# Stick-breaking attention with queries on partitions: a running product along the keys in place of logarithms and a triangle product

## The chip, the cores and the metric

One core of a Trainium2 chip. The metric is the device time of one launch in microseconds; it is compared as the median of runs, smaller is better.

## What is computed

One layer of a decoder trunk for a prompt of 1024 tokens and 8 sample tokens with a past of 2048 keys each. Only the stick-breaking attention is touched. For 8 heads of 64 dimensions, in f32:

```python
def stick_breaking(q, k, v, q_pos, k_pos, bias):
    z = jnp.einsum('bqhd,bkhd->bhqk', q, k) * HEAD_DIM ** -0.5
    z = z + bias[None, :, None, None]
    causal = (k_pos[None, :] < q_pos[:, None])[None, None]
    log_stay = jnp.where(causal, jax.nn.log_sigmoid(-z), 0.0)
    between = lax.cumsum(log_stay, axis=3, reverse=True) - log_stay
    a = jnp.where(causal, jnp.exp(jax.nn.log_sigmoid(z) + between), 0.0)
    return jnp.einsum('bhqk,bkhd->bqhd', a, v)
```

The weight of a key is the sigmoid of its own score, times sigmoid(-z) (the "stay factor") of every later key that the query may see. A query sees only keys strictly before it. Around it lie the input projection, windowed attention, gates, an output projection with routing, and 64 routed experts.

## The kernel before

The kernel is a sequence of phases, each a block of its own with a barrier behind it: `phase_project`, `phase_windows`, `phase_stick`, `phase_gate`, `phase_out_route`, `phase_experts`. Within a block each engine has its own written-out order of instructions, and semaphores are the only ties between engines.

`phase_stick` (L722) works on items. An item is a pair of heads `hp` (4 pairs), a block `c` of 512 queries and a block `kb` of 128 keys, keys on partitions and queries along the columns; keys go from the last block to the first, so that the sum over later keys can be carried. Blocks on the diagonal are 128, 256, 384 or 512 columns wide. There are 48 items: 24 of 512 columns and 8 each of 384, 256 and 128, each for both heads. For each item:

- TensorE: scores `pZ` (L1132, both heads in different rows of the array).
- VectorE: `low` = min(z + bias, 30) (L925). ScalarE: Exp (L1067) and Ln (L1084) on it, which gives the softplus. VectorE: `soft` = max of both (L900).
- GpSimd: masks `soft` on the diagonal (L1006) and adds it to the sum kept over later blocks, `later` (L1015, L1018). ScalarE and VectorE split `later` in a high and a low part (L1091, L909).
- TensorE: adds to `pZ` minus the sum over later keys of the same block by a product with a triangle of minus ones (L1146), and minus the kept sum by products with a matrix of minus ones (L1151).
- ScalarE: `prob` = Exp(pZ + bias) (L1061); GpSimd masks it on the diagonal (L1024). TensorE: values into `pO` (L1122). VectorE copies `pO` into `oT` when a block of queries is done (L915).

All engines walk over one list of ticks; in tick i TensorE scores item i+1, sums item i-1 and takes the values of item i-3, and so on. The eight sample tokens are woven in, one in five ticks: small operations of 128x128 on VectorE, ScalarE and GpSimd (L956 to L973, L1040 to L1049, L1075 to L1102), two TensorE products, and then four ticks with 16 value matmuls each (L1184) on 1 MB of cached values which SP loads in a ring of four (L870). From tick 10 on GpSimd also combines the outputs of the window groups for the late token tiles, 25 operations of 128x256 (L1031, L1034); before that VectorE and ScalarE make their weights (L931 to L949, L1094). TensorE turns the results at the end (L1161).

SP's order in the phase: page table, the sample's scores `s_z` (L858), values `v_rows` (L859), the window outputs (L863), the cached values, the first weights and activations of the gate phase (L874, L877), and behind the last scores the branch weights (L879, L880). In the gate phase (L1650) the first matmuls wait for a high/low split of these, and the branch weights are needed behind the first 48 matmuls. Constants for the stage are loaded, and one copied (L1499), in `phase_windows`; its end also loads the table of functions (L1500).

## Time and profile before

| | us |
|---|---|
| median of 3 runs (2139.99 to 2144.99) | 2140.8 |
| span of the profiled execution | 2142.2 |
| TensorE busy, share of the span | 1966.8, 92% |
| VectorE busy | 1328.2, 62% |
| ScalarE busy | 1035.2, 48% |
| GpSimd busy | 847.8, 40% |

The profile has no other time of that execution than its span, so the span stands for it. Busy times are of the whole kernel, so they are averages over phases with different limits; a phase has to be read in its own stretch. Durations of matmuls are modelled and overlap; the distance between the starts of two groups says more. Where two instructions of an engine overlap a little, the busy time divided by the count is shorter than the mean duration.

### The profile page before, as it was taken

How to read it: one execution, taken by the hardware profiler on the slowest of the kernel's cores; microseconds unless marked ns; L12 is line 12 of the kernel's file. 1: busy time of each engine (PE TensorE's matmuls, PEld its weight loads, DVE VectorE, ACT ScalarE, POOL GpSimd, SP SyncE). 2: the span in 40 equal slices, each digit the busy share in tenths (PEclk: the TensorE clock that was granted, in tenths of full speed). 3: DMA queues.
4: the chain of work that ended last, by engine and by line, in shares of the span. 5: the costliest groups of instructions: out<-in, count | busy, mean ns of one | idle time of the engine just before them, and what ended most of it. 6: DMA issues, size and time to landing. Idle time of an engine off the chain costs nothing. (4 is left out here: it accounts for less than half of the span.)

```text
span 2142.2 us, 37866 instructions
## 1 busy us (share of the span) xinstructions
PE 1966.8 (92%) x12744; PEld 1498.3 (70%) x12744; DVE 1328.2 (62%) x2267; ACT 1035.2 (48%) x1564; POOL 847.8 (40%) x788
## 2 busy tenths in 40 slices
PE   7999899978899989999899888999999999999994
PEld 5787778857444458888778554777777777777773
DVE  4389777785776662111257545777777777777772
ACT  6322133276666661111233203767676767666662
POOL 2111134252687731111005542455444546454452
PEclk9999899989899999999999899999999999999997
DMA  7488831083754547983253336999999999999995
GB/s 234 136 279 266 269 99 41 28 260 105 239 162 158 179 167 235 299 281 126 76 206 100 119 115 237 315 338 354 345 354 356 347 350 349 334 348 338 351 332 145
DMA packets 172371, 501.99 MB, mean 234 GB/s; under 512 B 26327, under 2 KB 73774, under 8 KB 145822
## 3 DMA queue, kind: packets, MB, share of 16 engines
q1 hardware_dynamic: 130070, 355.43, 45.8%
q0 software_dynamic: 31200, 79.17, 14.6%
q10 hardware_dynamic: 10992, 66.02, 9.1%
q8 instruction: 59, 0.97, 0.2%
q14 instruction: 50, 0.41, 0.1%
HBM read 438.01 MB, written 120.75 MB: 261 GB/s over the span
## 5 line engine op out<-in xcount | busy, mean ns | idle before, releaser
L2830 DVE TENSOR_TENSOR w_gu_lo<-turned,w_gu_hi 128x2048 fp32r<-128x2048 f32 x132 | 302.9, 2295 | 104.5 <-ACT w_gu_hi L2744 101.3
L2744 ACT ACTIVATE w_gu_hi<-turned 128x2048 fp32r<-128x2048 f32 x132 | 252.6, 1915 | 40.2 <-PEq L1992 40.2
L2592 POOL DMA_INDIRECT x_scratch<-turned,target x66 | 126.1, 1910 | 325.1 <-DMA x_scratch<-turned,target 279.9
L664 PE MATMUL pP<-wring,hT_hi 128*128 128x512 f32 (+2 forms) x520 | 206.5, 397 | 22.2 <-DVE wring L590 13.1
L2667 PE MATMUL pG_e<-w_gu_hi,xT_hi 128*128 128x512 f32 x528 | 216.8, 411 | 0.0
L2667 PE MATMUL pG_e<-w_gu_lo,xT_hi 128*128 128x512 f32 x528 | 209.9, 398 | 0.0
L2667 PE MATMUL pG_e<-w_gu_hi,xT_lo 128*128 128x512 f32 x528 | 209.6, 397 | 0.0
L666 PE MATMUL pP<-wring,hT_lo 128*128 128x512 f32 (+2 forms) x520 | 201.1, 387 | 0.0
L665 PE MATMUL pP<-wring,hT_hi 128*128 128x512 f32 (+2 forms) x520 | 201.0, 387 | 0.0
L2853 DVE TENSOR_TENSOR w_e_lo<-turned,w_e_hi 128x2048 fp32r<-128x2048 f32 x66 | 151.1, 2289 | 20.7 <-ACT w_e_hi L2758 20.7
L408 POOL TENSOR_TENSOR wring<-turned,wring 128x512 fp32r<-128x512 f32 (+1 forms) x43 | 68.7, 1623 | 227.0 <-ACT wring L444 226.7
L1711 PE MATMUL pG<-hg_hi,wg_hi 128*128 128x344 f32 x384 | 130.2, 339 | 6.2 <-DVE hg_lo L1772 6.2
L664 PEld LDWEIGHTS pP<-wring,hT_hi 128*128 128x128 f32 (+1 forms) x520 | 100.2, 193 | 46.3 <-DVE wring L590 14.6
L1798 POOL TENSOR_TENSOR turned<-halves 128x344 f32<-128x344 f32 x24 | 30.5, 1273 | 249.5 <-DVE halves L1791 249.5
L510 ACT ACTIVATE stage<-pP 128x512 f32<-128x512 f32 (+2 forms) x65 | 37.0, 569 | 186.0 <-PE pP L666 130.4
L2758 ACT ACTIVATE w_e_hi<-turned 128x2048 fp32r<-128x2048 f32 x66 | 125.7, 1904 | 0.0
L2667 PEld LDWEIGHTS pG_e<-w_gu_hi,xT_hi 128*128 128x128 f32 x528 | 100.4, 190 | 35.8 <-issue 12.7
L2770 ACT ACTIVATE silu_e<-pG_e 128x256 f32<-128x256 f32 x66 | 25.4, 384 | 206.4 <-PE pG_e L2667 206.4
L1791 DVE TENSOR_TENSOR halves<-turned,pG 128x344 f32<-128x344 f32 x48 | 22.4, 509 | 165.1 <-PE pG L1719 165.1
L1712 PE MATMUL pG<-hg_lo,wg_hi 128*128 128x344 f32 x384 | 123.7, 322 | 0.0
L1713 PE MATMUL pG<-hg_hi,wg_lo 128*128 128x344 f32 x384 | 123.6, 322 | 0.0
L2053 POOL DMA_INDIRECT table_scratch<-token_weight,dest x72 | 76.0, 1055 | 119.1 <-DVE turned L2309 99.3
(359 smaller groups left out, 4849.4 us busy)
## 6 DMA issues: line engine op xcount, KB each, us to landing
turned<-in_w_e_up SPq DMA_DIRECT2D x65, 1024.0 KB
turned<-in_w_e_down SPq DMA_DIRECT2D x65, 1024.0 KB
turned<-in_cache_sb_kv SPq DMA_DIRECT2D x256, 256.0 KB, 3.1
turned<-in_w_e_gate SPq DMA_DIRECT2D x64, 1024.0 KB
out<-in_cache_win_kv ACTq DMA_DIRECT2D x8, 4094.0 KB
turned<-in_w_in ACTq DMA_DIRECT2D x56, 256.0 KB, 6.4
turned<-in_w_in SPq DMA_DIRECT2D x16, 512.0 KB, 7.0
out<-in_cache_win_kv ACTq DMA_DIRECT2D x8, 1022.0 KB
```

The lines of the kernel that those rows point to most:

```text
L664: pe.matmul(pP[:m, b, :w], hi, w_hi(u), start=(c == 0), stop=False)
L665: pe.matmul(pP[:m, b, :w], hi, w_lo(u), start=False, stop=False)
L666: last = pe.matmul(pP[:m, b, :w], lo, w_hi(u), start=False, stop=(c == KC - 1))
L1711: pe.matmul(pG[:, i % 2, k, :NC], w_hi[:, r, c, :], hT_hi[:, c, cols], start=(c == 0), stop=False)
L1712: pe.matmul(pG[:, i % 2, k, :NC], w_hi[:, r, c, :], hT_lo[:, c, cols], start=False, stop=False)
L1713: last = pe.matmul(pG[:, i % 2, k, :NC], w_lo[:, r, c, :], hT_hi[:, c, cols], start=False, stop=(c == KC - 1))
L2592: pool.indirect_dma_start(sc["x2"], bass.IndirectOffsetOnAxis(ap=target[:, j, 0:1], axis=0), y[j], None, bounds_check=T - 1, oob_is_err=Fa ...
L2667: last = pe.matmul(pG[:, :, :], xs[:, r, c, :], ws[:, r, :, c, :], start=(n == 0), stop=(n == 3 * KC - 1))
L2744: act.activation(ghi[:, r, k, :, :].rearrange("p c f -> p (c f)"), w[:, r, k, :], ACT.Copy).then_inc(ghi_ready, 1)
L2758: act.activation(whi[:, r, :], w[:, r, 2, :], ACT.Copy).then_inc(whi_ready, 1)
L2830: dve.tensor_tensor(glo[:, r, k, :, :].rearrange("p c f -> p (c f)"), w[:, r, k, :], ghi[:, r, k, :, :].rearrange("p c f -> p (c f)").bitc ...
L2853: dve.tensor_tensor(wlo[:, r, :], w[:, r, 2, :], whi[:, r, :].bitcast(F32), ALU.subtract).then_inc(wlo_ready, 1)
```

## The change

Queries now lie on partitions and keys along the columns. An item is a head pair, a tile of 128 queries and a chunk of at most 512 keys; a tile with more than 512 keys has two chunks, the later one first. Again there are 24 items of 512 columns and 8 each of 384, 256 and 128. The last head pair takes its tiles in descending order. For each item:

- TensorE: scores; on a tile's first chunk one more single-pass product per head, identity times a mask of 0 and -2^100, adds the mask.
- ScalarE: `g` = sigmoid(z + bias) and `stay` = sigmoid(-z - bias), both from PSUM, two instructions each.
- VectorE: a running product of `stay` along the keys from last to first, one scan per head, started from the value of the chunk before (1 for the first).
- GpSimd: `g` times the running product shifted by one key, one instruction for both heads.
- TensorE: 128x128 transposes into `pA` (8 in a full item). ScalarE: copy to `aT`. TensorE: values, one product per 128 keys and head. ScalarE: copy of `pO` to `oT` when a tile is done.

The sample tokens are all done at the start in the same form: scores turned by transposes, one sigmoid per half of the keys for all 64 rows, the complement on GpSimd, scan and product on VectorE, transposes back in tick 3. Their value products keep their size and stand in ticks 4 to 42. Combination, turns and loads keep their order, but SP issues the sample's scores first. In the projection only the layout of these scores changes; in the windows phase fewer constants are loaded, the mask is made (VectorE) and rounded (ScalarE), and the table of Sigmoid is loaded in place of the one for Exp and Ln.

```diff
@@ phase_project
-                    dve.tensor_reduce(s_z[:, s, c * GP:(c + 1) * GP, :].rearrange("p a h -> p (a h)"),
-                                      prod.rearrange("p a (h d) -> p (a h) d", d=HD), AX_X, ALU.add).then_inc(s_score_ready, 1)
+                    dve.tensor_reduce(s_z[:, s, c * GP:(c + 1) * GP, :],
+                                      prod.rearrange("p a (h d) -> p a h d", d=HD), AX_X, ALU.add).then_inc(s_score_ready, 1)
@@ phase_stick, vector
+                dve.wait_ge(z_in, 16)
+                dve.tensor_tensor(s_z[:, :, :, :], s_z[:, :, :, :], bias[:, :].unsqueeze(1).unsqueeze(1).broadcast_to([P, NPAGES, NS, SBH]),
+                                  ALU.add).then_inc(s_z_ready, 1)
...
+                    j = i + 1
+                    if j < NI:
+                        it = items[j]
+                        at, w, n = it["at"], it["w"], it["n"]
+                        dve.wait_ge(stay_ready, j + 1)
+                        if not it["first"]:
+                            dve.wait_ge(scan_ready, j)
+                        if n >= 2:
+                            dve.wait_ge(a_ready, last_of[n - 2] + 1)
                         for par in range(2):
+                            row = prod[:, n % 2, par, :]
+                            last = dve.tensor_tensor_scan(row[:, at:at + w][:, ::-1], stay[:, j % RS, par, :w][:, ::-1], zero[:, :].broadcast_to([P, w]),
+                                                          row[:, at + w:at + w + 1], ALU.mult, ALU.add)
+                        last.then_inc(scan_ready, 1)
@@ phase_stick, gpsimd
+                for i in range(-2, TICKS):
+                    j = i + 1
+                    if 0 <= j < NI:
+                        it = items[j]
+                        at, w = it["at"], it["w"]
+                        pool.wait_ge(scan_ready, j + 1)
+                        part = g[:, j % RG, :, :w]
+                        pool.tensor_tensor(part, part, prod[:, it["n"] % 2, :, at + 1:at + w + 1], ALU.mult).then_inc(a_ready, 1)
+                    if i in (-1, 0):
+                        half = -i
+                        pool.wait_ge(s_g_ready, i + 2)
+                        if i == 0:
+                            pool.wait_ge(s_scan_ready, 1)
+                        pool.tensor_scalar(s_stay, s_g[:, half * HALF_KEYS:(half + 1) * HALF_KEYS], -1.0, 1.0, ALU.mult, ALU.add).then_inc(s_stay_ready, 1)
@@ phase_stick, scalar
+                    j = i + 2
+                    if j < NI:
+                        it = items[j]
+                        w, h = it["w"], 2 * it["hp"]
+                        act.wait_ge(z_ready, j + 1)
+                        if j >= RG:
+                            act.wait_ge(aT_psum, j - RG + 1)
                         for par in range(2):
+                            last = act.activation(g[:, j % RG, par, :w], pZ[:, j % 2, par, :w], ACT.Sigmoid, bias=bias[:, h + par:h + par + 1])
+                        last.then_inc(g_ready, 1)
...
+                        if j >= RS:
+                            act.wait_ge(scan_ready, j - RS + 1)
+                        for par in range(2):
+                            last = act.activation(stay[:, j % RS, par, :w], pZ[:, j % 2, par, :w], ACT.Sigmoid, bias=nbias[:, h + par:h + par + 1], scale=-1.0)
+                        last.then_inc(stay_ready, 1)
...
                     if 0 <= i < NI:
+                        w = items[i]["w"]
+                        act.wait_ge(aT_psum, i + 1)
+                        if i >= 2:
+                            act.wait_ge(pv_done, i - 1)
+                        act.activation(aT[:, i % 2, :, :w], pA[:, :, :w], ACT.Copy).then_inc(aT_ready, 1)
@@ phase_stick, tensor
+                for i in range(-2, TICKS):
+                    j = i + 2
                     if j < NI:
                         it = items[j]
+                        k0, w = it["k0"], it["w"]
+                        if j >= 2:
+                            pe.wait_ge(stay_ready, j - 1)
                         for par in range(2):
                             b = 64 * par
+                            last = pe.matmul(pZ[:, j % 2, par, :w], turned[b:b + 64, it["hp"], it["qt"] * P:(it["qt"] + 1) * P],
+                                             turned[b:b + 64, 4 + it["hp"], k0:k0 + w], start=True, stop=not it["first"], skip_group_check=True)
+                        if it["first"]:
+                            for par in range(2):
+                                last = pe.matmul(pZ[:, j % 2, par, w - P:w], ident_r[:, :], mask_r[:, :], start=False, stop=True, skip_group_check=True)
+                        last.then_inc(z_ready, 1)
...
+                    if 0 <= i < NI:
+                        pe.wait_ge(a_ready, i + 1)
...
+                        for k in range(items[i]["w"] // P):
+                            for par in range(2):
+                                last = pe.transpose(pA[:, par, k * P:(k + 1) * P], g[:, i % RG, par, k * P:(k + 1) * P], ident[:, :])
+                        last.then_inc(aT_psum, 1)
...
+                    j = i - 1
+                    if 0 <= j < NI:
+                        it = items[j]
+                        n = it["n"]
+                        pe.wait_ge(aT_ready, j + 1)
...
+                        blocks = it["w"] // P
+                        for k in range(blocks):
+                            for par in range(2):
+                                h = 2 * it["hp"] + par
+                                last = pe.matmul(pO[64 * par:64 * par + 64, :], v[:, it["k0"] // P + k, h * HD:(h + 1) * HD],
+                                                 aT[:, j % 2, par, k * P:(k + 1) * P], start=(it["first"] and k == 0),
+                                                 stop=(it["last"] and k == blocks - 1), skip_group_check=True)
+                        last.then_inc(pv_done, 1)
@@ phase_windows, scalar
-                act.wait_ge(stick["consts_in"], 64)
-                act.activation(stick["nones_r"][:, :], stick["nones"], ACT.Copy).then_inc(stick["nones_ready"], 1)
-                act.preload_act_table_set("natural_log_exp_and_others")
+                act.preload_act_table_set("sigmoid_and_others")
+                act.activation(stick["ident_r"][:, :], ident[:, :], ACT.Copy)
+                act.wait_ge(stick["not_earlier"], 1)
+                act.activation(stick["mask_r"][:, :], stick["mask"][:, :], ACT.Copy, scale=-LARGE).then_inc(stick["mask_ready"], 1)
```

## Rows read from the trace of the kernel before

**Rows 1.** The stage: length, then TensorE, its weight loads, VectorE, ScalarE, GpSimd; clock; DMA.
```profile
539.20:785.40 246.20, 228.79 (x1354) 112.14 (x1354) 172.40 (x296) 160.19 (x262) 180.94 (x200) 0.97 0.59 191
```

**Rows 2.** TensorE in order of time: start us, length us, line, output<-inputs, instructions.
```profile
655.80 1.07 PE L1184 MATMUL pS<-turned,s_prob 128*32 128x256 f32 x16
656.80 1.08 PE L1122 MATMUL pO<-prob,v_rows 128*64 128x512 f32 x4
...
767.84 1.13 PE L1132 MATMUL pZ<-turned 64*128 64x512 f32 x4 [0.35 <-ACT prob L1061]
768.90 1.98 PE L1146 MATMUL pZ<-soft,tri 128*128 128x512 f32 x4
770.32 1.03 PE L1151 MATMUL pZ<-later_hi,nones_r 128*128 128x512 f32 x2
...
771.65 0.95 PE L1169 MATMUL pS<-in_half,turned 128*128 128x1 f32 x8
```

**Rows 3.** The windows stage: TensorE in order of time, ScalarE's copy by line (us, ns).
```profile
503.75 1.09 PE L1411 MATMUL pT_d<-ident,e_win 128*128 128x128 f32 x8
504.77 1.09 PE L1424 MATMUL pO_d<-eT,v_win 128*64 128x128 f32 x16
...
L1478 ACT ACTIVATE eT<-pT_d 128x1024 f32<-128x1024 f32 x11 | 11.2, 1019 | 13.7 <-PE pT_d L1411 13.5
```

**Rows 4.** ScalarE by shape (count, busy us, mean ns); its Sigmoid and table load (min/median/max).
```profile
L1061 ACT ACTIVATE prob<-pZ,bias 128x512 f32<-128x512 f32 x48 | 30.2, 682 | 29.3 <-PE pZ L1151 29.3
L1061 ACT ACTIVATE prob<-pZ,bias 128x128 f32<-128x128 f32 x16 | 5.0, 364 | 5.2 <-PE pZ L1146 5.1
...
L1757 ACT ACTIVATE turned<-pG x48: 439/452/458, 801.3 to 1054.9; 128x344 f32<-128x344 f32 x48
L1757 ACT ACT_TABLE_LOAD  x1: 1283/1283/1283, 793.9 to 793.9; - x1
```

**Rows 5.** VectorE's scans and two-input subtraction (ns min/median/max, first and last start, shapes).
```profile
L2379 DVE TENSOR_TENSOR_SCAN base_row<-ones_r,stride_row x1: 291/291/291, 1075.6 to 1075.6; 128x64 f32<-128x64 f32 x1
L2325 DVE TENSOR_TENSOR_SCAN end<-ones_r,kinds x1: 426/426/426, 1243.8 to 1243.8; 128x128 f32<-128x128 f32 x1
L909 DVE TENSOR_TENSOR later_lo<-later,later_hi x40: 412/1191/3379, 544.5 to 776.5; 128x1024 fp32r<-128x1024 f32 x16, 128x256 fp32r<-128x256 f32 x8, 128x512 fp32r<-128x512 f32 x8, 128x768 fp32r<-128x768 f32 x8
```

**Rows 6.** GpSimd's addition by shape; it and VectorE's subtraction in order of time.
```profile
L1018 POOL TENSOR_TENSOR later<-later,soft 128x1024 f32<-128x1024 f32 x16 | 46.9, 2933 | 17.4 <-DVE soft L900 17.4
L1018 POOL TENSOR_TENSOR later<-later,soft 128x256 f32<-128x256 f32 x8 | 5.8, 725 | 0.0
...
644.67 1.21 DVE L909 TENSOR_TENSOR later_lo<-later,later_hi 128x1024 fp32r<-128x1024 f32 x1
644.83 3.28 POOL L1018 TENSOR_TENSOR later<-later,soft 128x1024 f32<-128x1024 f32 x1 [0.91 <-DVE soft L900]
650.61 3.27 POOL L1018 TENSOR_TENSOR later<-later,soft 128x1024 f32<-128x1024 f32 x1 [1.93 <-DVE soft L900]
...
771.82 2.36 POOL L1018 TENSOR_TENSOR later<-later,soft 128x1024 f32<-128x1024 f32 x1 [1.02 <-DVE soft L900]
771.92 3.34 DVE L909 TENSOR_TENSOR later_lo<-later,later_hi 128x1024 fp32r<-128x1024 f32 x1 [0.18 <-ACT later_hi L1091]
```

**Rows 7.** GpSimd's combination of the late tiles, by shape.
```profile
L1031 POOL TENSOR_TENSOR comb_late<-comb_late,wg_late 128x256 f32<-128x256 f32 x15 | 10.3, 686 | 0.0
```

**Rows 8.** DMA issues in the stage: KB each, us from issue to landing.
```profile
s_z<-sz_scratch SPq DMA_DIRECT2D x1, 512.0 KB, 3.7
turned<-in_w_br_b SPq DMA_DIRECT2D x1, 1024.0 KB, 10.0
```

**Rows 9.** TensorE at the start of the gate phase, in order of time.
```profile
790.95 0.66 PE L1711 MATMUL pG<-hg_hi,wg_hi 128*128 128x344 f32 x1 [6.23 <-DVE hg_lo L1772]
```

**Rows 10.** Busy time, clock and DMA by stretch in the windows stage (columns as rows 1).
```profile
460.00:480.00 20.00, 17.26 (x159) 11.67 (x158) 18.53 (x166) 17.83 (x73) 15.29 (x29) 1.00 1.03 344
...
520.00:540.00 20.00, 14.16 (x124) 11.18 (x126) 9.76 (x42) 11.62 (x31) 7.95 (x15) 0.83 0.23 75
```

## What the time after is expected to be, and why

> **What bounds the kernel now.** I read the busy time by stretch first [rows 1]. The stick-breaking stage is one stretch between two barriers, from 539.2 us (first score matmul) to 785.2 us (last copy), 246 us long. In it TensorE is busy 228.8 us, VectorE 172.4, ScalarE 160.2 and GpSimd 180.9. The reader is to see that no engine is far from full, but TensorE is fullest, and that DMA, at 191 GB/s, is not. The stages around it are other programs behind barriers: the next one's first matmul stands at 790.95, 6.2 us after this stage's last, and its release comes from VectorE's split of operands loaded during this stage [rows 9]. So what this stage gives or takes is passed on to the end one for one, as long as those loads land in time.
>
> Then I read TensorE's order of work in full-width items (512 columns) by the distance between starts, because the durations of matmuls overlap [rows 2]: scores 1.06 us (767.84 to 768.90), triangle product 1.42, products of the kept sum 1.33 (770.32 to 771.65), values 1.01 (the 1.08 less the overlap of 0.07), and 1.00 for the sample's values in four ticks of five. That is 5.8 us with the sample's part and 4.8 without. Two full items follow each other by 5.8 us (GpSimd's addition at 644.83 and 650.61) [rows 6], so TensorE's own chain is what ends last, with GpSimd's sum close behind.
>
> **What goes.** The triangle product and the kept-sum products (2.8 us of TensorE in a full item), Exp and Ln, the two VectorE passes over PSUM, the hi/lo split, and GpSimd's sum and its two masks. The cut into items is new, but its widths are the same: 24 items of 512 columns, and 8 each of 384, 256 and 128 for both heads of a pair.
>
> **What comes, engine by engine, for a full item.**
>
> TensorE: scores 1.06 as before; eight 128x128 transposes, which in the windows stage take 1.02 from start to start; sixteen value records with 64-column weights, again 1.09 long there, so 1.02 [rows 3]; the sample's values 1.00 as before [rows 2]. Sum 4.1 us in four ticks of five and 3.1 otherwise, against 5.8 and 4.8. The mask product on a first item is two single-pass 128-column matmuls; four single-pass ones of 512 columns take 1.33 us [rows 2], so I take 0.3 (estimate) in 32 of 48 items. TensorE falls from first place.
>
> ScalarE: four sigmoids from PSUM. The nearest rows are Exp from PSUM with a bias in the same widths: busy time by count is 0.63 us for 512 columns and 0.31 for 128 [rows 4], and 0.52 and 0.42 between. Four to an item are 24 x 2.52 + 8 x (2.08 + 1.68 + 1.24), 100 us. A Sigmoid row with 344 columns has 0.45 us, no more than that [rows 4]. The copy of the transposed weights out of PSUM is 1.02 us for 1024 columns [rows 3]; narrower by the slope of rows 4 it is 0.81, 0.60 and 0.38, and all copies make 39. Thirty-two output copies of 128 columns at 0.28 (estimate, a little under Exp's 0.31) make 9. The sample's part and the rest are about 7. Exp of the late combination now stands between sigmoids, so it needs two table loads at 1.28 us [rows 4], 2.6 us. One load at the start of the next stage falls away, where ScalarE is not what is waited for. Sum 158 us, 3.8 us in a full item.
>
> VectorE: the running product is a scan. Two rows have 64 and 128 columns with 0.291 and 0.426 us [rows 5]: 2.1 ns for each further column, twice the slope of a two-input elementwise operation (0.41 us at least, for 256 columns, and 1.21 for 1024, 1.04 ns each) [rows 5, 6]. A 512-column scan is then 1.23 us, 384 gives 0.96, 256 gives 0.70. Two in an item: 2.46, 1.93, 1.39 and 0.85 us. All: 92 us.
>
> GpSimd: one product over both heads. Its addition of the same shape and inputs in the kernel before takes 2.36 us for 1024 columns when undisturbed and 0.725 for 256 [rows 6], which makes 1.81 and 1.27 between. All: 87 us.
>
> **The term that decides: VectorE and GpSimd do not run these at the same time.** The sixteen 1024-column additions on GpSimd have a mean of 2.93 us, and single ones read 2.36 or 3.27. In one case VectorE's two-input operation started at 644.67 and took 1.21; GpSimd's started at 644.83 and took 3.28. In another GpSimd started at 771.82 and took 2.36; VectorE's started at 771.92 and took 3.34, which is 2.13 more than its own 1.21 [rows 6]. Whichever starts first has both inputs to itself and the other waits it out. The scan also has two inputs in SBUF (the stay factors and a broadcast zero), so I take scans and products as one queue. No row of this trace shows a scan beside GpSimd; the bounds are nothing (the scan leaves GpSimd alone) and the whole of it (as the elementwise row), and I take the whole, as the nearest row.
>
> The Trainium skill, GPSIMD Engine Reference, Key points, says that GpSimd shares its SBUF interfaces with VectorE and contends with VectorE instructions that have two SBUF inputs. That speaks against this change, because it names the number of inputs and not the operation; by it the scan would block too, and the sum would be the one below. The trace agrees for elementwise operations, 2.36 against 3.27 us.
>
> Sum of this queue. Full item 2.46 + 2.36 = 4.82; less the overlap of consecutive instructions (the 2.36 holds the inputs for about 2.13, the pair of scans shares some 0.1) it lies between 4.5 and 4.8, and I take 4.7. The others: 3.65, 2.6, and for 128 columns 1.9, where ScalarE (4 x 0.31 + 0.38 + 0.28) is longer than the 1.58 of the queue. 24 x 4.7 + 8 x (3.65 + 2.6 + 1.9) = 113 + 65 = 178 us.
> - Late combination on GpSimd, 15 operations for 10.3 us [rows 7] and 10 like them for 7: unchanged, 17 us. Until now it lay in GpSimd's free time; here it stands in the full queue.
> - The sample, now all at once at the start: the bias addition 1.2, two scans over 1024 columns 2 x 2.3, two products 2 x 1.2, two one-input GpSimd passes of about 1.3 (estimate, a good half of the two-input 2.36): 11 us. In the kernel before it was spread in free time over all ticks.
> - The start: VectorE's first instruction of weight waits for the sample's scores, whose DMA lands in 3.7 us [rows 8] and is issued first now. VectorE's first scan is queued behind it, and so is everything after: 4 us.
> - VectorE's small work on the weights of the groups, two-input and mostly 0.2 to 1.2 us each: 4 us.
> - The end: the last item is the narrowest now (128 columns) and nothing but a transpose, two copies and the combination's last turns stand behind it: 3 us.
>
> Total 178 + 17 + 11 + 4 + 4 + 3 = 217 us against 246: 29 us less, rounded to 30 since some of the small VectorE work falls into gaps.
>
> **What lies around.** In the windows stage two constants less are loaded, one 128x128 addition comes on VectorE and one 0.3 us copy on ScalarE; these stand at the phase's end, so up to 0.4 us may be added (estimate from the 0.31 us of ScalarE's 128 columns). The layout of the sample's scores in the projection changes a stride of 32 outputs per reduction, which I cost at nothing beside its 2048 inputs. The DMA of the stage, 191 GB/s x 246 us = 47 MB, would take 137 us at the 344 GB/s of a stretch before it [rows 1, 10], well under 217. The branch weights are issued with the last scores, which is only some 6 us before the stage's end now, and the later one took 10.0 us to land [rows 8]; they are needed behind the 48 first gate matmuls, which begin 6 us past the end [rows 9] and take some 8 (estimate from 0.16 each of the 1.33 us for four wider ones), so they stay hidden. If the stage ran 8 us shorter still, they would be too.
>
> The profiled span is 2142.2 us; the median of the runs is 2140.8, 1.4 less. 2142.2 - 30 = 2112.2, and brought to the median 2111.
>
> **Rivals.**
> 1. The scan doesn't block GpSimd. Then the loop of dependences decides: three items are in flight, and one turn of it is scan 2.46, product 2.36, transposes 1.02, sample values 1.0, values 1.02, next scores 1.06, four sigmoids 2.52, and six handovers of 0.1 to 0.2, 12.3 us, or 4.1 an item. 24 x 4.1 + 8 x (3.3 + 2.6 + 1.9) = 161, with 17 for the sample, start and end 178: 68 us less, 2073. For it: the scan takes a column every 2.1 ns, so its inputs are idle half of the time. Against it: the waits in rows 6 are those of whole instructions. 0.12.
> 2. The blocking lengthens the loop too. If VectorE's next scan gets in front of GpSimd's product each time, the turn is 12.3 + 2.4, and with a fold and a combination step in it 15.8, that is 4.9 to 5.3 an item. Stage 222 to 236, time 2117 to 2131. For it: VectorE is released by ScalarE alone and so is early. 0.13.
> 3. Slower: TensorE's clock. The work on TensorE is cut from 5.8 to 4.1 us and stands in gaps now. The granted clock is 0.83 in the stretch 520 to 540, where TensorE was busy 14.2 of 20 us, but 1.00 from 460 to 480, where the same kind of transposes and narrow value matmuls kept it busy 17.3 of 20 [rows 10]. At the lower level (1.2 of 2.4 GHz) a full item costs TensorE 8.2 us with the sample's part, more than every other engine; 24 x 7.8 (its mean with four fifths of the sample's part) + 8 x 11.7 + 20 = 301, that is 55 us more, 2196. It decides from a full item of 5.9 us, so from a mean clock of about 0.7. 0.07.
> The Trainium skill, TensorE: Matmul & The Clock Gate, Part 4, says that transposes do not count as TensorE being busy in the same way, so that the high clock doesn't engage for them. By it this rival would be likely here; rows 10 speak against it for a mix like this one.
> 4. Slower as well: the scan runs over reversed columns, and no row has a negative stride. Were it to cost twice its time, 92 us would be added: 2203. 0.04.
> 5. No change: half gains with a start that is much longer than 4 us, such as the sample's chain (transpose, sigmoid, complement, scan, product, all serial and twice) holding TensorE until 570. It would have to cost 25 us more than I give it. 0.07.
>
> **How the numbers follow.** The forecast (2098 to 2125) has 0.57, rival 1 0.12, rival 2 0.13, no change 0.07, slower 0.11. A difference of 0.3%, 6.4 us, is about what a measurement of this kernel can tell from none. Faster 0.82, same 0.07, slower 0.11. From 2070 (rival 1) to 2140 (the whole of rival 2 and a part of no change) some 0.82 to 0.85 is held.
>
> **What would show it.** In the profile after: stage 217 us; scans of 1.23 us for 512 columns where GpSimd is idle; GpSimd's 1024-column product in two durations, 2.4 and up to 4.8, or VectorE's scans stretched by some 2.1; VectorE plus GpSimd busy with waits inside filling the stage; TensorE's gaps before transposes released by GpSimd; clock 1.00 past the first 20 us. I am wrong if products stay at 2.36 beside running scans, if the clock stands at 0.5 in the stage, or if full items repeat slower than every 5.9 us.

## The result, and the profile after

The changed kernel takes 2109.8 us (median of 4 runs, 2104.3 to 2114.4) against 2142.9 us for the kernel before on the same chip: a ratio of 0.984, 95% interval 0.981 to 0.987. Run once more on another chip it took 2101.0 us (2093.1 to 2107.2) against 2132.3, ratio 0.986 (0.981 to 0.990). The forecast was 2111 us, 30 less; the measurements say 33 and 31 less.

The profiled execution has a span of 2108.6 us. Its stick-breaking stage (columns as in [rows 1]; stretch, length, then busy time of TensorE, its weight loads, VectorE, ScalarE and GpSimd, clock, DMA share, GB/s):

```profile
535.81:747.94 212.13, 184.31 (x1738) 114.89 (x1738) 155.21 (x130) 144.72 (x283) 115.78 (x79) 0.91 0.69 217
```

and the same stage in the profile of the second chip:

```profile
539.00:758.20 219.20, 192.65 (x1738) 119.26 (x1738) 152.81 (x130) 144.99 (x283) 116.14 (x79) 0.88 0.67 214
```

The stage took 246.2 us before [rows 1], and takes 212.1 or 219.2 now, 215.7 in the mean; the forecast was 217. Two profiles of one program differ by 7.1 us here, so a single stage length tells nothing finer than that. What stands ahead of the stage took 535.8 and 539.0 us (539.2 before), what stands behind it 1360.7 and 1346.3 (2142.2 - 785.4 = 1357 before); these parts are nearly the same program, and their scatter isn't the change's.

The costliest groups of the stage, by shape (busy us, mean ns of one, idle before and its releaser):

```profile
L915 DVE TENSOR_TENSOR_SCAN prod_stick<-stay_stick,prod_stick,zero_stick 128x512 f32<-128x512 f32 x48 | 76.0, 1625 | 19.0 <-ACT stay_stick L1011 18.6
L970 POOL TENSOR_TENSOR g_stick<-g_stick,prod_stick 128x1024 f32<-128x1024 f32 x24 | 54.8, 2282 | 55.2 <-DVE prod_stick L915 55.2
L1078 PEld LDWEIGHTS pA<-ident,g_stick 128*128 128x128 f32 x288 | 33.5, 150 | 37.1 <-POOL g_stick L970 31.1 <-issue 5.8
L1011 ACT ACTIVATE stay_stick<-pZ,nbias_stick 128x512 f32<-128x512 f32 x48 | 30.4, 692 | 0.0
L1004 ACT ACTIVATE g_stick<-pZ,bias 128x512 f32<-128x512 f32 x48 | 30.4, 683 | 19.5 <-PE pZ L1048 10.3 <-PE pZ L1052 9.2
L1026 ACT ACTIVATE aT_stick<-pA 128x1024 f32<-128x1024 f32 x24 | 24.8, 1035 | 7.6 <-PE pA L1078 7.6
L983 POOL TENSOR_TENSOR comb_late<-comb_late,wg_late 128x256 f32<-128x256 f32 x15 | 14.6, 974 | 0.0
L986 POOL TENSOR_TENSOR comb_late<-comb_late 128x256 f32<-128x256 f32 x10 | 12.1, 1215 | 0.0
```

TensorE's transposes (L1078) wait for GpSimd's product, GpSimd waits for VectorE's scans, and VectorE waits 19 us for ScalarE at this width. Every engine waits for the next one, so the list of waits alone names no bound. The scans carry the clue. Undisturbed they take 1.25 us, but their mean is 1.63. In order of time:

```profile
625.46 1.25 DVE L915 TENSOR_TENSOR_SCAN prod_stick<-stay_stick,prod_stick,zero_stick 128x512 f32<-128x512 f32 x1
...
638.68 6.57 DVE L915 TENSOR_TENSOR_SCAN prod_stick<-stay_stick,prod_stick,zero_stick 128x512 f32<-128x512 f32 x3
640.33 2.35 POOL L970 TENSOR_TENSOR g_stick<-g_stick,prod_stick 128x1024 f32<-128x1024 f32 x1 [1.16 <-DVE prod_stick L915]
642.64 1.53 POOL L983 TENSOR_TENSOR comb_late<-comb_late,wg_late 128x256 f32<-128x256 f32 x1
642.73 1.83 PE L1078 MATMUL pA<-ident,g_stick 128*128 128x128 f32 x8 [1.33 <-POOL g_stick L970]
645.33 2.35 POOL L970 TENSOR_TENSOR g_stick<-g_stick,prod_stick 128x1024 f32<-128x1024 f32 x1 [1.16 <-DVE prod_stick L915]
```

Of the three scans that start at 638.68, one takes 3.42 us:

```profile
L915 DVE TENSOR_TENSOR_SCAN prod_stick<-stay_stick,prod_stick,zero_stick x3: 1566/1567/3421, 638.7 to 643.7; 128x512 f32<-128x512 f32 x3
```

It was issued beside the product of 640.33 and is longer than its own 1.25 by 2.17, nearly the whole product. The combination step at 642.64 is stretched in turn, from 0.61 to 1.53. Two full items follow each other by 5.0 us here, of which 0.3 is the combination step; the forecast had 4.7 without it.

Counting together the time in which VectorE or GpSimd or both show an instruction gives 189.6 of the 212.1 us, and 189.9 of 219.2 on the second chip. In the middle of the stage (562 to 735 us) it is 161.5 of 173. The queue of the two is nearly full, but not quite. This count holds the waiting too, so it does not name a bound by itself: in the kernel before it was 229.2 of 246.2 us, with TensorE busy 228.8. And TensorE is still the busiest single engine of the changed stage, 184 us. Only experiments can tell which of them holds it.

### The profile page after: what moved, and what is told of

Same layout as the page of the kernel before. It is cut to its first block and busy times, and to the rows that moved or that the text cites. A ratio compares the mean times of both kernels' runs of the same rounds, so it can differ in the third digit from the quotient of the medians.

```text
span 2108.6 us, 38215 instructions
## 1 busy us (share of the span) xinstructions
PE 1926.4 (91%) x13128; PEld 1501.8 (71%) x13128; DVE 1306.8 (62%) x2102; ACT 1018.5 (48%) x1585; POOL 791.4 (38%) x667
## 3 DMA queue, kind: packets, MB, share of 16 engines
q8 instruction: 62, 1.02, 0.2%
## 5 line engine op out<-in xcount | busy, mean ns | idle before, releaser
L2527 POOL DMA_INDIRECT x_scratch<-turned,target x66 | 135.4, 2051 | 319.9 <-DMA x_scratch<-turned,target 267.3
L915 DVE TENSOR_TENSOR_SCAN prod_stick<-stay_stick,prod_stick,zero_stick 128x512 f32<-128x512 f32 (+3 forms) x96 | 134.8, 1451 | 37.8 <-ACT stay_stick L1011 37.3
```

The source lines that it names most:

```text
L915: last = dve.tensor_tensor_scan(row[:, at:at + w][:, ::-1], stay[:, j % RS, par, :w][:, ::-1], zero[:, :].broadcast_to([P, w]), row[:, at ...
L2527: pool.indirect_dma_start(sc["x2"], bass.IndirectOffsetOnAxis(ap=target[:, j, 0:1], axis=0), y[j], None, bounds_check=T - 1, oob_is_err=Fa ...
```

## The experiments

Two theories were set against each other. By the queue theory, scans and products exclude each other and the sum of both sets the stage. By the loop theory, three items in flight and the turn of dependences (scan, product, transposes, copy, scores, sigmoids) set it, and the stretched instructions only fill idle time. A third candidate is TensorE. "Stage" below is the stage's length in the profiled execution, one profile for each run. Since two profiles of one program gave 212.1 and 219.2, a difference of stages below 7 us tells nothing by itself.

**Product on VectorE.** The product stands right behind its scans and GpSimd has only the late combination and the sample's complements:

```
 dve.tensor_tensor_scan(...)                      # both heads
+dve.wait_ge(scan_ready, j + 1)
+dve.tensor_tensor(part, part, prod[...], ALU.mult).then_inc(a_ready, 1)
...
-pool.tensor_tensor(part, part, prod[...], ALU.mult).then_inc(a_ready, 1)
```

> The product of g and the running product moves from GpSimd to VectorE, straight behind its scan; everything else stays. Theory (one queue): VectorE's scans and GpSimd's products wait for each other, so the stage (212 us, of which one of the two engines is at work in 190) is held by the sum of both. On VectorE a full product costs 1.21 us in place of 2.0 to 2.4, all of them together about 40 us less, so the queue falls under ScalarE's 155 us and the stage falls to about 180: 2078. Rival (loop): what holds the stage is the turn of dependences with three items in flight; it gets 1.15 us shorter in a full item, 0.4 an item, so 10 to 13 us less: 2097 to 2100. Second rival (two engines are better than one): VectorE now does 92 + 45 us of work in order and waits for ScalarE in front of each scan, and the stage gets longer, 220 or more: 2118.

Measured: 2096.2 us, ratio 0.978 (0.973 to 0.983), stage 197.7, so 14.4 less than the changed kernel (18 less than the mean of its two profiles). VectorE's and GpSimd's common time fell from 189.6 to 163.3 us, more than the stage did. So part of what the queue gave up went into another limit. The queue theory's 180 us missed by 18; the loop theory's 10 to 13 us less and 2097 to 2100 us come much nearer.

**Transposes behind the values.** TensorE does the sample's values and the values of the item before first, and waits for the product only then:

```
-[transposes of item i, waits for a_ready]
 [sample's values]
 [values of item i - 1]
+[transposes of item i, waits for a_ready]
```

(The few transposes of the late combination move behind with them.)

> Only the order on TensorE changes: the sample's values and the values of the item before come ahead of the transposes of this item, so that they run in its wait for the product, and the next scores follow the transposes at once. Theory (one queue): the queue of scans and products is not touched, the stage stays at 208 to 212 us and the time within 4 us of 2110. Rival (loop): the turn of 12.3 us loses the 2.0 us of both value steps, 0.67 an item in full ones, so the stage falls by 15 to 25 us: 2085 to 2095.

Measured: 2096.5 us, ratio 0.977 (0.972 to 0.981), stage 203.0, 9.1 less (13 less than the mean of the two). No work was taken from the queue (185.1 us in common), so the queue alone wasn't what held the stage; the turn of the loop held it too. The evidence is one profile, 2 us outside the scatter, and the ratio to the kernel before, 0.977 against the changed kernel's 0.984 and 0.986, whose intervals just touch. Neither theory has its number.

**Both together.**

> Both edits: product on VectorE, and the value steps ahead of the transposes on TensorE. Theory (one queue): with the queue gone ScalarE (155 us) and the turn are next, and the order now counts: stage 165 to 172 us, 2063 to 2070, more than the sum of the two edits alone. Rival (loop): the sum of the two alone, 25 to 35 us less: 2075 to 2085.

Measured: 2083.9 us, ratio 0.973 (0.969 to 0.978), stage 194.2. The queue theory's 165 to 172 us failed; the time is in the loop theory's 2075 to 2085, the stage's gain of 17.9 below its 25 to 35. The two edits gave 14.4 and 9.1 alone and 17.9 together. Their sum is 23.5, but a lack of 5.6 us is inside the scatter of 7, so that they add up to less is likely and not shown. The medians of the three on one chip are 2096.2, 2096.5 and 2083.9 us, so either edit alone leaves some 12 us to the other, with ranges that overlap in part. Once more beside the changed kernel, on one chip:

> The changed kernel itself once more, so that it and the next one stand side by side on one chip: 2105 to 2114 us, stage 210 to 214.

> The version with the product on VectorE and the transposes behind the values once more, beside the changed kernel: 2080 to 2092 us, which would be 18 to 30 us less than the changed kernel, stage 192 to 196. If the gain seen before was one of the chip and not of the edit, the two stand within 6 us of each other.

Measured: 2101.0 us (2093.1 to 2107.2) for the changed kernel, with a stage of 219.2 (both outside what was expected), and 2081.1 (2073.6 to 2085.3) for this version, ratios to before 0.986 (0.981 to 0.990) and 0.978 (0.975 to 0.981); the runs of the two don't overlap. It is 20 us faster than the changed kernel, and faster than both kernels of this case. Its stage:

```profile
536.80:730.20 193.40, 179.54 (x1738) 109.95 (x1738) 158.83 (x178) 144.40 (x283) 33.18 (x31) 0.95 0.77 243
```

and two stretches of 20 us of it, then its TensorE in order of time:

```profile
590.00:610.00 20.00, 20.00 (x207) 12.29 (x201) 19.00 (x18) 14.71 (x32) 19.37 (x19) 1.00 0.72 217
610.00:630.00 20.00, 20.00 (x206) 11.23 (x208) 19.83 (x19) 16.54 (x32) 6.11 (x5) 1.00 0.77 236
```

```profile
677.98 1.05 PE L1085 MATMUL pS<-turned,s_z 128*4 128x256 f32 x16
678.96 1.09 PE L1102 MATMUL pO<-aT_stick,v_rows 128*64 128x128 f32 x16
679.98 1.09 PE L1116 MATMUL pA<-ident,g_stick 128*128 128x128 f32 x8
681.00 1.13 PE L1044 MATMUL pZ<-turned 64*128 64x512 f32 x4
682.06 1.05 PE L1085 MATMUL pS<-turned,s_z 128*4 128x256 f32 x16
```

TensorE is busy without a gap here, and in 119.0 of the 120 us from 590 to 710, at the full clock; a full tick is 682.06 - 677.98 = 4.08 us. So in the middle of this version's stage the bound is TensorE, 4.1 us to a full item. That would also be why the two edits give less together than apart; no run took work from TensorE here to show it.

**Without the sample's weights.**

> Leaves out the making of the sample tokens' weights at the start of the stage (bias, transposes both ways, sigmoid, complement, scan and product), so the sample outputs are wrong; their value products stay and use the raw scores. By the sum of the forecast this is 11 us of queue and 4 us of waiting for their load: the stage falls from 212 to about 197. If the start is a chain instead that holds TensorE until the weights are back, 20 us or more go; if it is hidden behind the main items, under 6.

Measured: 2104.1 us, stage 204.6, that is 7.5 less than the changed kernel's 212.1. **Without the late combination on GpSimd:**

> The changed kernel without the 25 operations of the late combination on GpSimd, so the outputs of the late tiles are wrong. One queue: they stand in it with 17 us, so the stage falls by 12 to 17 us, from 212 to 195 to 200. Loop: they are in GpSimd's free time, the stage falls by 4 us at most.

Measured: stage 205.6, 6.5 less. (Its time, 2124.5 us, has 1379.9 us behind the stage, some 19 more than any other run here; that isn't the stage's, so only the stage is read.) Both values are of the size of the scatter between two profiles, 7 us, and each is a single run. Set against the changed kernel's second profile (219.2) they would be 14.6 and 13.6. So each part probably costs less than the 15 and 17 us that the sum gave it, and what either costs stays open. Neither run has what the forecast's sum wanted (about 197, and 195 to 200).

**The prompt's items alone, zero in SBUF or in PSUM.** To take away the exclusion without touching work, one operand has to leave SBUF. In the changed kernel no PSUM bank is free of TensorE's writes, so the comparison was made in a pair that leaves out the sample and the late turns. (Whether a spare column of a bank that TensorE also writes would do, no run tried.) The edit between the two:

```
-zero = sb("zero_stick", [P, 1])
+zero = pS[:, 511:512]
```

> The stage with its prompt items alone: the sample tokens' weights, value products, folds and gathers are left out, and the turns of the late combination on TensorE too, so sample outputs and late tiles are wrong. It frees one PSUM bank and is the base for the next run. One queue: own times of the scans (about 92 us) and products (about 80) and nothing else but the combination's 17 in it, stage 185 to 192 us. Loop: the turn loses the sample's values (1.0 of 12.3 us, 0.33 an item) and the start, stage 180 to 188. The two are not told apart here but by the next run.

> As the run before, but the scan's second input, the broadcast zero, is read from the freed PSUM bank, so that the scan has one input in SBUF and not two. If the number of SBUF inputs makes the two engines exclusive (the forecast), 512-column scans are never over 1.4 us and 1024-column products never over about 2.4, both run at once, and the stage falls from the bare 185 to 190 to what ScalarE (some 145 us) and the turn without waits (11.3 us, 3.8 an item) allow: 155 to 170. If the scan blocks GpSimd for another reason, the long ones (2.3 to 3.4 us) stay and the stage is within 3 us of the run before.

Measured: 2086.3 us with a stage of 189.8, and 2059.1 with 169.8. The VectorE and GpSimd groups, first with zero in SBUF:

```profile
L907 DVE TENSOR_TENSOR_SCAN prod_stick<-stay_stick,prod_stick,zero_stick 128x512 f32<-128x512 f32 x48 | 79.8, 1704 | 19.1 <-ACT stay_stick L987 18.5
L952 POOL TENSOR_TENSOR g_stick<-g_stick,prod_stick 128x1024 f32<-128x1024 f32 x24 | 59.0, 2457 | 43.7 <-DVE prod_stick L907 43.7
L959 POOL TENSOR_TENSOR comb_late<-comb_late,wg_late 128x256 f32<-128x256 f32 x15 | 16.6, 1106 | 0.0
```

then in PSUM:

```profile
L907 DVE TENSOR_TENSOR_SCAN prod_stick<-stay_stick,prod_stick,pS 128x512 f32<-128x512 f32 x48 | 58.8, 1268 | 41.9 <-ACT stay_stick L987 41.9
L952 POOL TENSOR_TENSOR g_stick<-g_stick,prod_stick 128x1024 f32<-128x1024 f32 x24 | 52.9, 2204 | 50.7 <-DVE prod_stick L907 50.6
L959 POOL TENSOR_TENSOR comb_late<-comb_late,wg_late 128x256 f32<-128x256 f32 x15 | 9.2, 613 | 0.0
```

The same 48 scans fall from a mean of 1.70 us to 1.27. With zero in SBUF 24 of them take over 1.4 us, up to 3.31; with PSUM the longest takes 1.28. The combination steps fall from 1.11 to 0.61 us. This is the exclusion, shown by moving one column of zeros, and the move is worth 20 us of this stage. TensorE's mean clock rose with it, from 0.87 to 0.92, and its busy time fell from 150.2 to 141.2 us for the same work; how much of the 20 us came by way of that isn't separated.

**The same pair with the transposes behind the values.**

> The kernel with the prompt's items alone (stage 189.8 us), zero in SBUF, TensorE's order changed as above. The same parts are left out. The union of VectorE and GpSimd is 177 of those 190 us. If the queue of both engines holds the stage here, the order gives only the free 12 us or less: 178 to 188. If the loop of dependences holds it and the waits in scans and products only fill it, the stage gets shorter by 14 or more: 165 to 176.

> The kernel with the prompt's items alone and the scan's zero in PSUM (stage 169.8 us), and TensorE's order changed as well: in each tick the values of the item before stand ahead of the transposes of this one. Left out as in that kernel: the sample's weights and values, the late turns, so the sample's attention rows are not the reference's. No VectorE instruction waits for GpSimd here, so the queue of both engines (153.7 us) can't hold the stage. If the loop of dependences does, taking the wait of the values behind the transposes out of it saves up to the 1.02 us of a full item's values per tick, at a third to the whole of it: 48 ticks x 0.3 to 0.8 = 14 to 38 less, but not below ScalarE's 138 us with its waits, so 145 to 156. If instead what is left is TensorE's own time at a lowered clock or ScalarE, the order changes nothing: 167 to 171.

Measured with zero in SBUF: stage 189.9, no less than 189.8. In its middle (560 to 715 us) VectorE or GpSimd is at work in 151.7 of 155 us. The order gives nothing here, while the zero in PSUM gives 21.3 us in this pair too (189.9 to 168.6). So without the sample's values on TensorE the queue holds the stage, and the loop theory falls for this kernel. With zero in PSUM: 168.6 against 169.8, again nothing, and not the 145 to 156 of the loop. What may hold it then can be read in the windows of that kernel:

```profile
630.00:650.00 20.00, 16.57 (x141) 10.48 (x142) 11.22 (x12) 17.88 (x39) 12.25 (x12) 1.00 0.75 234
650.00:670.00 20.00, 18.14 (x157) 11.41 (x154) 14.01 (x13) 18.84 (x33) 15.70 (x11) 1.00 0.75 229
670.00:690.00 20.00, 18.56 (x162) 12.18 (x162) 11.74 (x13) 18.29 (x35) 10.09 (x7) 1.00 0.71 224
```

ScalarE (fourth number with a count) is busy 17.9 to 18.8 of 20 us and is the fullest engine or level with TensorE. My reading is that these two are the next limits; no run took work from them in this kernel.

**The stay factor as 1 - g on GpSimd** instead of the second sigmoid, on top of the version with both edits:

```
-act.activation(stay[...], pZ[...], ACT.Sigmoid, bias=nbias[...], scale=-1.0)
+pool.tensor_scalar(stay[...], g[...], -1.0, 1.0, ALU.mult, ALU.add)
```

(TensorE then waits for `g` in place of `stay` before it writes over the scores.)

> Takes the kernel with the product on VectorE and the new order on TensorE (stage 194 us) and undoes the second sigmoid: the stay factor is 1 - g, one pass on GpSimd over both heads. ScalarE loses 50 of its 145 us. If ScalarE were what holds that stage, it would fall to 175. By the forecast's queue GpSimd's passes (about 1.05 us for 1024 columns, 40 in all) come into the queue with VectorE's 159, 199 in all, and the stage rises to 200 to 210. If TensorE holds it (its own work is 166 us at the full clock, and some of it runs at the lower), it stays at 192 to 197.

Measured: 2095.0 us, stage 197.3, 3.1 more than with the second sigmoid, though ScalarE's busy time falls from 144.6 to 100.2 us. VectorE's and GpSimd's common time rose from 161.5 to 185.5: the edit refilled the queue. So it brought nothing as a whole, and the 175 us of a stage held by ScalarE did not come; but since it loads one limit while it frees another, it doesn't show by itself that ScalarE held nothing. The windows above, with TensorE full and ScalarE at 14.7 and 16.5 of 20 us, speak for TensorE.

## Why the prediction held, and where it didn't

**TensorE, 4.1 us to a full item: right,** 4.08 in the version in which nothing else holds it. Transposes 1.02 (678.70 to 679.72), values 1.03, and the mask product 0.27 to 0.49 from start to start where nothing waits (0.3 predicted). "TensorE falls from first place" holds only in this sense, that the common time of the two others, 189.6 us, is a little more than its 184; with both edits it is the bound of the stage's middle. Its total was put too low: half of rival 3's 301 us would be 150 at the full clock, and the version with both edits shows 179.5 us busy at a mean clock of 0.95. One part is in the sum for the narrower items, 11.7 us at the lower level: 3.1 us scaled to their widths makes 4.65 for the three, the sample's values 2.4, so 14.1 at that level.

**ScalarE: the terms right, the sum 13 too high.** Sigmoids 101.4 us (100 predicted), weight copies 39.6 (39), output copies 9.1 (9), two table loads 1.28 each. Yet the busy time of the stage is 144.7 us and not 158: the busy times by shape leave out the overlap within a shape only, and instructions of different shapes overlap by another 13 us, which the sum should have had from distances between starts.

**VectorE, 92 us of scans: right.** Undisturbed they take 1.25, 0.99, 0.72 and 0.46 us (1.23, 0.96, 0.70, 0.43 predicted), and with zero in PSUM all of them are 91.9 us. In the changed kernel they show 135 us, since some 43 us of waiting stand inside them.

**GpSimd's products, 87 us: right,** 85.4 measured. The 1024-column one reads 2.00 or 2.35 where nothing disturbs it, and only 2.28 in the mean: GpSimd is seldom the one that waits, VectorE is.

**One queue: right as a mechanism, and not the whole of the bound.** Zero in PSUM shows the exclusion. That the queue takes 4.7 us to an item fits the 5.0 seen with a combination step. But the sum took it for the only limit, and moving the transposes, which takes no work from the queue, gave 9 us. In the changed kernel a transpose that waits for a late product holds the sample's values and the values behind it on TensorE. So the loop of rivals 1 and 2 has a part in it, though not by rival 2's mechanism, in which scans get in front of the products each time: the 1024-column products have a mean of 2.28 us and hardly wait.

**The additions to the queue: too high.** 17 us for the combination and 11 + 4 for the sample and the start were taken in full; leaving them out gave 6.5 and 7.5, each within the scatter of one profile. Part of that work then lies in the queue's gaps, which the sum hadn't. The combination steps themselves show 26.7 us busy (974 and 1215 ns each) against 16.5 of their own: there the waiting is on GpSimd's side. So that 217 came out so near 215.7 is in part luck: two errors cancel, as far as these runs tell, too much for the additions, and nothing for the gaps in the queue (11.5 us from 562 to 735 in the first profile, 17.3 from 562 to 745 in the second). What held is the queue as the largest term.

**The clock: the expectation wrong, though it decided nothing.** I expected 1.00 past the first 20 us. The stretches say otherwise, in the changed kernel and in its second profile:

```profile
550.00:570.00 20.00, 14.51 (x98) 9.73 (x94) 15.60 (x11) 10.68 (x23) 11.11 (x5) 0.66 0.63 211
570.00:590.00 20.00, 18.92 (x194) 11.07 (x190) 15.23 (x16) 16.66 (x30) 7.18 (x4) 1.00 0.67 205
...
690.00:710.00 20.00, 18.33 (x188) 11.60 (x188) 15.74 (x10) 13.48 (x22) 14.18 (x7) 0.91 0.60 184
```

```profile
570.00:590.00 20.00, 19.76 (x188) 10.98 (x186) 11.29 (x11) 14.26 (x28) 6.61 (x5) 0.91 0.50 159
590.00:610.00 20.00, 17.53 (x182) 10.98 (x180) 15.06 (x21) 14.79 (x28) 9.99 (x8) 0.91 0.59 184
610.00:630.00 20.00, 18.53 (x158) 10.69 (x158) 12.07 (x10) 12.09 (x27) 9.60 (x8) 0.83 0.60 186
```

Single pieces at the lower level (1.2 of 2.4 GHz) keep coming back, after stretches in which TensorE stood waiting for products: one begins at 642.9, behind the wait of 1.33 us that ends at 642.73. The transposes from 642.73 above stand in one: 1.83 us for eight instead of 1.09. The mean is 0.91 and 0.88, against 0.97 before [rows 1]. The second profile has 0.03 less clock, 8.3 us more TensorE time for the same 1738 matmuls, the same queue (189.9 against 189.6) and a stage 7.1 us longer. So the clock may account for the difference between the two profiles; whether it made the stage longer, or longer waits made the clock lower, the rows don't separate, and no run shows what it takes of the gain. The stage's mean never came near the 0.7 from which rival 3 would have decided, though single stretches did (0.66 from 550 to 570). The Trainium skill (TensorE: Matmul & The Clock Gate, Part 4) says that transposes don't count as TensorE being busy in the same way and that the high clock doesn't engage for them. In this mix, 288 transposes of weights among the 1738 matmuls, it stands at 1.00 in 6 of the 9 stretches of 20 us from 550 to 730, and in 3 of them in the second profile; what a stage of transposes alone would do no run here shows.

**The rivals.** Rival 1 (the scan leaves GpSimd alone) falls with the stretched scans. Whether its 178 us would have come without the exclusion no run shows for the full stage; the bare kernel with zero in PSUM has 169.8 with the sample left out. Rival 4 falls: a reversed scan of 512 columns takes 1.25 us, against 1.23 from the slope of the straight ones. Of rival 5, the start: the first transpose of weights stands at 549.20, and the making of the sample's weights is worth 7.5 us (14.6 by the second profile), not 25.

**Around the stage.** The first gate matmul stands 5.7 us behind the end of the stage's last copy (it was 5.7) and is released by the same split of operands as in [rows 9]:

```profile
747.75 0.19 DVE L953 COPY oT<-pS 128x32 f32<-128x32 f32 x1 [4.76 <-ACT odT L1034]
...
753.65 0.66 PE L1646 MATMUL pG<-hg_hi,wg_hi 128*128 128x344 f32 x1 [6.22 <-DVE hg_lo L1707]
```

The branch weights, issued at 740.95 and 741.38, took 7.8 and 9.8 us and stayed hidden: they had landed by 751.2, ahead of the first gate matmul. (The 48 matmuls in front of them take 10.1 us and not 8. The 0.16 each was misread: 1.33 us for four of 512 columns is 0.33 each, 0.22 for 344.)

## What to carry to other kernels

Before moving an elementwise operation to GpSimd "beside" VectorE, look whether VectorE's instructions read two operands from SBUF. In all the runs here where they did, the two engines' times added up. What took the sum apart was one of VectorE's operands in PSUM; the same product on VectorE, at about half its duration (1.25 us against 2.28 in the mean, for 1024 columns), made the sum smaller. On an in-order engine, put the work that is ready ahead of the wait for the work that isn't. And when two edits each gain, run them together: here 14 and 9 us made 18, and a third engine, at 4.1 us to the item, had become full.

## What the runs showed of the hardware

A scan counts as an instruction with two SBUF inputs even where one of them is a single column of zeros broadcast along the row, and though it takes a column only every 2.1 ns. It waits for the whole of a GpSimd product (1.25 us becomes 3.42), and GpSimd waits for it in turn. With that column in PSUM, all 48 scans of 512 columns took 1.25 to 1.28 us and none waited. The Trainium skill, GPSIMD Engine Reference, Key points, ties the contention to VectorE instructions with two SBUF inputs; the runs agree, by 20 us of a 190 us stage for that one operand.

GpSimd need not have two inputs itself. In the version with the stay factor on GpSimd, a pass with one SBUF input takes its own 1.05 us, and the scan that starts 0.01 us ahead of it 2.12 in place of 1.25:

```profile
633.31 1.05 POOL L973 TENSOR_SCALAR stay_stick<-g_stick 128x1024 f32<-128x1024 f32 x1 [1.01 <-ACT g_stick L1007]
L915 DVE TENSOR_TENSOR_SCAN prod_stick<-stay_stick,prod_stick,zero_stick x1: 2121/2121/2121, 633.3 to 633.3; 128x512 f32<-128x512 f32 x1
```

A short instruction waits as long as a long one. An elementwise operation over 20 columns, in the kernel with zero in PSUM:

```profile
573.89 2.00 POOL L952 TENSOR_TENSOR g_stick<-g_stick,prod_stick 128x1024 f32<-128x1024 f32 x1 [2.31 <-DVE prod_stick L907]
573.91 2.01 DVE L915 TENSOR_TENSOR top_late<-top_late,comb_late 128x20 f32<-128x20 f32 x1
575.95 0.36 DVE L918 TENSOR_TENSOR wg_late<-comb_late,top_late 128x20 f32<-128x20 f32 x3
```

The first takes 2.01 us, exactly as long as the product beside it; the three behind it take 0.36 together.

GpSimd's product over 1024 columns has two undisturbed durations, 2.00 and 2.35 us (10 and 14 of the 24 with zero in PSUM). What decides between them none of the runs tells.
